# VectorE instead of GpSimd forms the low parts of the weights in the linear stages, and areas move to multiples of 512 bytes

## The chip, the cores and the metric

The kernel runs on one core of one Trainium2 chip. The metric is the device time of one execution in microseconds, taken as the median of several executions. Four engines compute: TensorE (PE, with its weight loads as PEld), VectorE (DVE), ScalarE (ACT) and GpSimd (POOL). SyncE (SP) issues the loads of the weights.

## The reference, cut to what matters

Two transformer-like blocks run one after the other on x of 512 tokens by 1024 features, in float32. Each has RMS norm, an input projection, mixers, an output projection that is added to x, a second norm, and a feed-forward part. Block one mixes by pooling and sparse attention, block two by a gated delta rule and banded attention. The stages on which the change acts are these:

```
# block one
h = rms_norm(x, ffn_norm_g)
gate_pre, val = split(h @ w_up, 2)                  # 1024 -> 2 x 2816
x = x + (silu(causal_dwconv(gate_pre, conv_w, conv_b)) * val) @ w_down
# block two
h = rmsnorm(x, norm_mix_w);  proj = h @ w_in
qkv = silu(causal_dwconv_2(concat([qa, ka, va]), conv_qkv_w))      # 4 taps
...
x = x + mix @ w_out
h = rmsnorm(x, norm_ffn_w)
u = causal_dwconv_2(h @ w_up, conv_ffn_w) + conv_ffn_b             # 3 taps, gate and value
gate, up = split(u, 2)
x = x + (silu(gate) * up) @ w_down
```

## The kernel before, in words

Activations lie with the features on the 128 partitions and the 512 tokens along the free dimension. Every product with a weight is made of three products of the faster float32r type: both the weight and the activation are split in a high and a low part, and high x high, high x low and low x high are summed in PSUM (lines 1452 to 1454, each a 128x128 weight slice against 128x512).

The weights come in 228 chunks, each the 8 slices (11 in the down projections) that make one output tile or half of one. w_raw, w_hi and w_lo have two slots each. For a chunk c, SyncE loads w_raw once w_lo of chunk c - 2 is made (line 508, the function load); ScalarE copies it to w_hi once TensorE is done with chunk c - 2 (semaphore chunk_done, line 679); GpSimd subtracts w_lo = w_raw - w_hi (line 590, the function low, semaphore lo_ready); TensorE waits for lo_ready and multiplies. Everybody prepares chunk c + 2 behind chunk c (the function ahead). While TensorE multiplies chunk c + 1, both parts of chunk c + 2 have to be made.

The stages and their numbers of chunks stand in the list STAGES: in1 15 and fill1 16 (input projection of block one, the latter interleaved with attention), mix1 8, out1 8, up1 44 (22 tiles of a gate chunk and a value chunk), down1 16 (8 tiles of two large chunks), in2c 12 (the convolution stage), in2z 5, fill2 28 (interleaved with the delta rule and attention), mix2 8, out2 8, up2 44, down2 16. In the trace up1 is 421 to 663 us, in2c 786 to 858, in2z 858 to 888 and up2 1316 to 1584. The tiles run in hardware loops of two tiles per iteration; the first two and the last two or so of a stage are unrolled.

What VectorE does behind a chunk, by the order of its instruction stream:

- up stages (function ffn): for the gate chunk it multiplies the bank by rms_inv into t_raw (line 1012), then applies three taps into t_gate (TENSOR_SCALAR at 1068, the second step at 1070, the third at 1073). In up1 the value chunk is only multiplied (into t_val); in up2 it gets the same convolution into t_val. Then t_gate x t_val (line 1089) once ScalarE has made the silu of t_gate, and act_lo = t_gate - act_hi (line 995) once ScalarE has made act_hi.
- in2c: multiplied by rms_inv into cv_raw, then four taps into cv (1288, 1291 three times); ScalarE makes the silu.
- out and down stages (function residual): adds the bank to X, makes h_lo (line 1001) and adds the square to sq_sum (line 1008), both behind ScalarE.
- mix stages (function merge): two gate products, their sum, and mix_lo behind ScalarE's mix_hi.
- in2z: multiplies by rms_inv (copy_tiles).

TensorE waits, apart from lo_ready, for a bank to be read (conv_done, cv_done, x_done). Behind the first chunk of a norm's stage it makes the mean of squares; ScalarE turns it into rms_inv, for which VectorE waits before its first multiplication.

Buffers in SBUF are placed by hand: weights, X, h_hi, h_lo, constants and parameters first, and then an arena in which the areas of the stages overlap.

Of the kernel before, what the change touches and what calls it, by code (L numbers as in the profile page):

```python
# [24 lines left out]
ALU = mybir.AluOpType  # L25
# [3 lines left out]
P = 128  # L29
T = 512  # L30
D = 1024
DK = D // P
# [117 lines left out]
def lin(a, b, i):  # L150

    return a + b * i if isinstance(i, int) else i * b + a
# [39 lines left out]
def two_blocks(nc, t_in, out):  # L192
# [10 lines left out]
    with ctx:  # L203
        kb = 1024
        base = -(-nc.sbuf_base // 64) * 64

# [7 lines left out]
        at = 0  # L214
# [10 lines left out]
        rms_inv = sb("rms_inv", [P, T], F32, at); at += T * 4  # L225
        arena = at
        arena_size = (nc.sbuf_usable_end - base - arena) // 64 * 64
# [260 lines left out]
        def ahead(c, q_kt):  # L488
# [4 lines left out]
            return (Chunk(n, 0, 0, None, False), SIZES[n]) if n < NCHUNK else (None, 0)  # L493

        def wait(eng, s, value):
            if not isinstance(value, int) or value > 0:
                eng.wait_ge(s, value)
# [88 lines left out]
        def _(pool):  # L586
            def low(c, kt):

                pool.wait_ge(hi_ready, c.count(1))
                pool.tensor_tensor(w_lo[:, c.slot, 0:kt * P], w_raw[:, c.slot, 0:kt * P],  # L590
                                   w_hi[:, c.slot, 0:kt * P], ALU.subtract).then_inc(lo_ready, 1)

            def split(name):
                n, per, kt = INFO[name]
                for i, j in units(pool, n):
                    for q in range(per):
                        c2, kt2 = ahead(chunk(name, i, j, q), kt)
                        if c2:
                            low(c2, kt2)

            def lows(name, plan, total):

                state = [0]

                def serve(*at):
                    upto = (plan[at][0] if at else total) // PIECES
                    while state[0] < upto:
                        low(*ahead(chunk(name, state[0] // 2, state[0] % 2), DK))
                        state[0] += 1
                return serve  # L610

            low(Chunk(0, 0, 0, None, False), DK)
            low(Chunk(1, 0, 0, None, False), DK)
            split("in1")
            pool.wait_ge(copied["in1"], 15)
# [19 lines left out]
            serve()  # L635
            for name in ("mix1", "out1", "up1", "down1", "in2c", "in2z"):
                split(name)
            pool.wait_ge(copied["in2z"], 5)
            pool.memset(gb_rows[:, :], 0.0).then_inc(blk_zero, 1)
            serve = lows("fill2", FILL2, FILLED2)  # L640
# [27 lines left out]
            serve()  # L668
            for name in ("mix2", "out2", "up2", "down2"):
                split(name)  # L670

# [321 lines left out]
        def _(dve):  # L993
# [34 lines left out]
            def residual(name, n):  # L1028
                per = INFO[name][1]
                for i, j in units(dve, DK):  # L1030
                    m = lin(j, 2, i)
                    dve.wait_ge(chunk_done, chunk(name, i, j, per - 1).count(1))
                    dve.tensor_tensor(X[:, m, :], X[:, m, :], bank(ACC + j), ALU.add).then_inc(x_done, 1)  # L1033
                    gained(n, m, j, isinstance(i, int) and m == 0)

            def copy_tiles(name, dst):
                for i, j in units(dve, INFO[name][0]):
                    dve.wait_ge(chunk_done, chunk(name, i, j).count(1))
                    scaled(dst[:, lin(j, 2, i), :], bank(ACC + j)).then_inc(copied[name], 1)

            def merge(name, b, sg, mt, mix_hi, mix_lo):
                for i, j in units(dve, DK):
                    m = lin(j, 2, i)
# [8 lines left out]
                    wait(dve, mix_hl[b], m)  # L1052
                    dve.tensor_tensor(mt[:, 2, :], mt[:, 0, :], mt[:, 1, :], ALU.add).then_inc(mixed[b], 1)
                    dve.wait_ge(mix_hh[b], lin(j + 1, 2, i))
                    sub(mix_lo[:, m, :], mt[:, 2, :], mix_hi[:, m, :]).then_inc(mix_hl[b], 1)

            def ffn(name, b, steps):
# [18 lines left out]
                for i, j in units(dve, FK):  # L1076
                    f = lin(j, 2, i)
                    val = t_val[:, j, :]
                    dve.wait_ge(chunk_done, chunk(name, i, j, 0).count(1))
                    conv(t_gate[:, j, :], bank(ACC), t_raw[:, 0, :], f, steps * j, i, j)  # L1080
                    dve.wait_ge(chunk_done, chunk(name, i, j, 1).count(1))
                    if b == 0:
                        wait(dve, gated[b], lin(j - 1, 2, i))
                        scaled(val, bank(ACC + 1)).then_inc(conv_done[b], 1)
                    else:
                        conv(val, bank(ACC + 1), t_raw[:, 1, :], lin(FK + j, 2, i), steps * j + 4, i, j)
                    dve.wait_ge(conv_done[b], lin(steps * j + steps, 2 * steps, i))
                    dve.wait_ge(silu_done[b], lin(j + 1, 2, i))
# [191 lines left out]
            for i, j in units(dve, 12):  # L1280
# [8 lines left out]
                for k in range(1, 4):  # L1289
                    dve.wait_ge(cv_done, lin(5 * j + k + 1, 10, i))  # L1290
                    dve.scalar_tensor_tensor(dst[:, k:], raw[:, 0:T - k], taps[:, t, 3 - k:4 - k], dst[:, k:],  # L1291
                                             ALU.mult, ALU.add).then_inc(cv_done, 1)
            copy_tiles("in2z", p2a[:, 12:17, :])

# [670 lines left out]
```

## Time and profile before

| what | value |
|---|---|
| median of 3 runs | 1731.11 us |
| lowest, highest | 1723.51, 1732.45 us |
| the profiled execution | 1725.94 us |
| its span, first to last instruction | 1724.0 us |
| TensorE, VectorE, ScalarE, GpSimd busy | 94%, 58%, 33%, 37% |
| mean granted clock of TensorE | 0.99 |
| w_lo subtractions on GpSimd | 228, 588.6 us busy |
| w_hi copies on ScalarE | 228, 250.4 us busy |

Engines work in parallel and meet at semaphores. Matmuls are pipelined: each 128x512 one is shown as some 0.39 us, while the next starts 0.23 us after it, so a TensorE that is shown 100% busy is one that never pauses. What an engine waited for stands in brackets behind a row. A granted clock of 1.00 is 2.4 GHz, 0.50 is 1.2 GHz.

### The profile page before, as it was taken

The numbers are of one execution on the slowest core, as the hardware profiler recorded it, in microseconds if no ns is written. First come the engines' busy times: TensorE is split into PE (matmuls) and PEld (weight loads), VectorE is DVE, ScalarE is ACT, GpSimd is POOL, SyncE is SP. The second block draws the span as 40 slices with busy tenths as digits, with TensorE's granted clock in tenths as the row PEclk, the third lists the DMA queues.
The fourth block names the chain that finished last, engine by engine and source line by source line (L and its number), as shares of the span: only waits on it lengthen the run. The fifth ranks groups of instructions, "written<-read, shape, count | busy, mean of one in ns | idle before, by whom it ended". The sixth has DMA issues, their size and how long they took to land.

```text
span 1724.0 us, 21757 instructions
## 1 busy us (share of the span) xinstructions
PE 1628.1 (94%) x7872; PEld 1277.9 (74%) x7872; DVE 995.8 (58%) x1295; ACT 568.8 (33%) x906; POOL 641.3 (37%) x274
## 2 busy tenths in 40 slices
PE   6997899999999999999999999999999999998997
PEld 4876666678888887887776798666688777777885
DVE  5146566576777775326924732245566888888223
ACT  5132455544322222223234223135444222222221
POOL 3452211144444444443433541131244444443432
PEclk9998999999999999999999999999999999999998
DMA  6421212142222223222222211252232222223231
GB/s 225 156 87 55 67 56 71 60 161 96 98 97 95 93 96 109 98 83 86 86 92 92 74 38 37 78 208 82 98 137 96 85 85 85 85 85 104 84 101 66
DMA packets 49845, 163.10 MB, mean 95 GB/s; under 512 B 5088, under 2 KB 5352, under 8 KB 49648
## 3 DMA queue, kind: packets, MB, share of 16 engines
q1 hardware_dynamic: 46544, 156.09, 26.4%
q10 hardware_dynamic: 3232, 6.08, 1.0%
q8 instruction: 44, 0.72, 0.2%
q14 instruction: 25, 0.20, 0.0%
HBM read 148.50 MB, written 13.65 MB: 94 GB/s over the span
## 4 chain that ended last, share of the span: by engine, by line
PE 69%; DVE 20%; issue 5%; ACT 4%; DVEq 1%; POOL 0%; DMA 0%; ACTq 0%
PE banks L1452 19%; PE banks L1454 18%; PE banks L1453 18%; DVE t_val L1073 3%; DVE t_gate L1068 3%; DVE cv L1291 2%; DVE t_raw L1012 2%; PE banks L1543 2%; PE banks L1569 2%; PE banks L1552 1%; DVE t_gate L1070 1%; PE banks L1773 1%; PE banks L1762 1%; DVE t_val L1070 1%; DVE t_gate L1089 1%
## 5 line engine op out<-in xcount | busy, mean ns | idle before, releaser
L590 POOL TENSOR_TENSOR w_lo<-w_raw,w_hi 128x1024 fp32r<-128x1024 f32 (+1 forms) x228 | 588.6, 2581 | 1020.8 <-ACT w_hi L679 1020.8
L1452 PE MATMUL banks<-h_hi,w_hi 128*128 128x512 f32 x1312 | 535.8, 408 | 49.6 <-POOL w_lo L590 31.5
L1454 PE MATMUL banks<-h_hi,w_lo 128*128 128x512 f32 x1312 | 514.2, 392 | 0.0
L1453 PE MATMUL banks<-h_lo,w_hi 128*128 128x512 f32 x1312 | 513.8, 392 | 0.0
L679 ACT ACTIVATE w_hi<-w_raw 128x1024 fp32r<-128x1024 f32 (+1 forms) x228 | 250.4, 1098 | 432.4 <-PE banks L1454 397.5
L1452 PEld LDWEIGHTS banks<-h_hi,w_hi 128*128 128x128 f32 x1312 | 247.6, 189 | 127.0 <-issue 53.0
L1454 PEld LDWEIGHTS banks<-h_hi,w_lo 128*128 128x128 f32 x1312 | 247.4, 189 | 53.5
L1453 PEld LDWEIGHTS banks<-h_lo,w_hi 128*128 128x128 f32 x1312 | 247.8, 189 | 51.2 <-issue 4.8
L1452 PE MATMUL banks<-act_hi,w_hi 128*128 128x512 f32 x352 | 140.7, 400 | 4.1 <-DVE t_raw L1012 3.2
L1453 PE MATMUL banks<-act_lo,w_hi 128*128 128x512 f32 x352 | 140.2, 398 | 0.0
L1454 PE MATMUL banks<-act_hi,w_lo 128*128 128x512 f32 x352 | 140.1, 398 | 0.0
L1033 DVE TENSOR_TENSOR X<-X,banks 128x512 f32<-128x512 f32 (+1 forms) x32 | 22.0, 687 | 176.4 <-PE banks L1454 176.4
L1068 DVE TENSOR_SCALAR t_gate<-t_raw,params 128x512 f32<-128x512 f32 x44 | 94.2, 2140 | 11.9 <-DVE t_raw L1012 11.6
L744 ACT ACTIVATE t_gate<-t_gate 128x512 f32<-128x512 f32 x44 | 27.8, 633 | 196.7 <-DVE t_gate L1073 196.7
L1001 DVE SCALAR_TENSOR_TENSOR h_lo<-X,params,h_hi 128x512 fp32r<-128x512 f32 (+1 forms) x32 | 71.1, 2221 | 36.4 <-ACT h_hi L718 36.4
L995 DVE TENSOR_TENSOR act_lo<-t_gate,act_hi 128x512 f32 (+1 forms) x44 | 66.7, 1515 | 39.2 <-ACT act_hi L747 39.2
L1452 PEld LDWEIGHTS banks<-act_hi,w_hi 128*128 128x128 f32 x352 | 66.8, 190 | 21.1 <-DVE t_raw L1012 3.6
L778 ACT ACTIVATE at_p<-at_sm,cols 128x128 f32<-128x128 f32 (+3 forms) x96 | 53.2, 555 | 87.0 <-DVE cols L1108 49.5
L1454 PEld LDWEIGHTS banks<-act_hi,w_lo 128*128 128x128 f32 x352 | 66.8, 190 | 16.3
L1453 PEld LDWEIGHTS banks<-act_lo,w_hi 128*128 128x128 f32 x352 | 66.9, 190 | 16.0
L1073 DVE SCALAR_TENSOR_TENSOR t_val<-t_raw,params,t_val 128x510 f32<-128x510 f32 x22 | 59.5, 2704 | 2.8
L747 ACT ACTIVATE act_hi<-t_gate 128x512 f32 (+1 forms) x44 | 27.8, 632 | 96.7 <-DVE t_gate L1089 96.7
(273 smaller groups left out, 1988.7 us busy)
## 6 DMA issues: line engine op xcount, KB each, us to landing
w_raw<-in_w_up SPq DMA_DIRECT2D x88, 512.0 KB, 3.4
w_raw<-in_w_fill SPq DMA_DIRECT2D x44, 512.0 KB, 3.5
w_raw<-in_w_down SPq DMA_DIRECT2D x32, 704.0 KB, 4.0
late_scratch<-stage SPq DMA_DIRECT2D x44, 256.0 KB, 2.1
w_raw<-in_w_mix SPq DMA_DIRECT2D x16, 512.0 KB, 4.3
sg<-late_scratch SPq DMA_DIRECT2D x16, 512.0 KB, 3.8
w_raw<-in_w_out SPq DMA_DIRECT2D x16, 512.0 KB, 3.5
w_raw<-in_w_in SPq DMA_DIRECT2D x15, 512.0 KB, 3.5
```

The source lines that it names most:

```text
L590: pool.tensor_tensor(w_lo[:, c.slot, 0:kt * P], w_raw[:, c.slot, 0:kt * P], w_hi[:, c.slot, 0:kt * P], ALU.subtract).then_inc(lo_ready, 1)
L679: act.activation(w_hi[:, c.slot, 0:kt * P], w_raw[:, c.slot, 0:kt * P], ACT.Copy)\
L778: act.activation(a.p[:, s % 2, half, 0:w], a.sm[:, half, 0:w], ACT.Exp, bias=a.nbias[:, c:c + 1], scale=DH ** -0.5, accum_out=a.sums[:, c: ...
L995: return dve.tensor_tensor(out_, a, b, ALU.subtract)
L1001: dve.scalar_tensor_tensor(h_lo[:, m, :], X[:, m, :], gains[:, m + DK * n, :], h_hi[:, m, :], ALU.mult, ALU.subtract).then_inc(hl_done, 1)
L1012: return dve.tensor_tensor(dst, src, rms_inv[:, :], ALU.mult)
L1068: dve.tensor_scalar(dst, raw, w(2), w(3), ALU.mult, ALU.add).then_inc(conv_done[b], 1)
L1070: dve.scalar_tensor_tensor(dst[:, 1:], raw[:, 0:T - 1], w(1), dst[:, 1:], ALU.mult, ALU.add)\
L1073: dve.scalar_tensor_tensor(dst[:, 2:], raw[:, 0:T - 2], w(0), dst[:, 2:], ALU.mult, ALU.add)\
L1452: pe.matmul(dst, w_h, hi[:, kr, :], start=first and n == 0, stop=False)
L1453: pe.matmul(dst, w_h, lo[:, kr, :], start=False, stop=False)
L1454: mm = pe.matmul(dst, w_l, hi[:, kr, :], start=False, stop=last and n == len(ks) - 1)
```

## The change

The function low, which subtracts, becomes one that can be issued on either engine, and next_low issues the one for the chunk two ahead. In in1, fill1 and fill2 it stays with GpSimd, and so do the first two chunks behind each fill stage. In mix1, out1, up1, down1, in2c, in2z, mix2, out2, up2 and down2 VectorE issues it: behind the convolution or the multiplication of the chunk, in residual behind sq_sum (and for all but a tile's last chunk, before the bank is awaited), in merge between the sum and mix_lo. These are 169 of the 228 subtractions. merge on VectorE now begins with a wait until GpSimd's two subtractions for the first two mix chunks are made, and GpSimd waits before it clears gb_rows until VectorE's for the first two fill2 chunks are made. The number of each kind of operation stays the same. Apart from this, the first buffer and the arena begin at multiples of 512 bytes instead of 64.

```diff
-        base = -(-nc.sbuf_base // 64) * 64
+        base = -(-nc.sbuf_base // 512) * 512
...
-        arena = at
+        arena = at = -(-at // 512) * 512
...
+        def low(eng, c, kt):
+
+            eng.wait_ge(hi_ready, c.count(1))
+            eng.tensor_tensor(w_lo[:, c.slot, 0:kt * P], w_raw[:, c.slot, 0:kt * P],
+                              w_hi[:, c.slot, 0:kt * P], ALU.subtract).then_inc(lo_ready, 1)
+
+        def next_low(eng, name, i, j, q=0):
+            c2, kt2 = ahead(chunk(name, i, j, q), INFO[name][2])
+            if c2:
+                low(eng, c2, kt2)
...
-            for name in ("mix1", "out1", "up1", "down1", "in2c", "in2z"):
-                split(name)
             pool.wait_ge(copied["in2z"], 5)
+            pool.wait_ge(lo_ready, BASE["fill2"] + 2)
             pool.memset(gb_rows[:, :], 0.0).then_inc(blk_zero, 1)
...
-            for name in ("mix2", "out2", "up2", "down2"):
-                split(name)
...
                 for i, j in units(dve, DK):
                     m = lin(j, 2, i)
+                    for q in range(per - 1):
+                        next_low(dve, name, i, j, q)
                     dve.wait_ge(chunk_done, chunk(name, i, j, per - 1).count(1))
                     dve.tensor_tensor(X[:, m, :], X[:, m, :], bank(ACC + j), ALU.add).then_inc(x_done, 1)
                     gained(n, m, j, isinstance(i, int) and m == 0)
+                    next_low(dve, name, i, j, per - 1)
...
             def merge(name, b, sg, mt, mix_hi, mix_lo):
+                dve.wait_ge(lo_ready, BASE[name] + 2)
...
                     dve.tensor_tensor(mt[:, 2, :], mt[:, 0, :], mt[:, 1, :], ALU.add).then_inc(mixed[b], 1)
+                    next_low(dve, name, i, j)
...
                     conv(t_gate[:, j, :], bank(ACC), t_raw[:, 0, :], f, steps * j, i, j)
+                    next_low(dve, name, i, j, 0)
...
                         conv(val, bank(ACC + 1), t_raw[:, 1, :], lin(FK + j, 2, i), steps * j + 4, i, j)
+                    next_low(dve, name, i, j, 1)
...
                     dve.scalar_tensor_tensor(dst[:, k:], raw[:, 0:T - k], taps[:, t, 3 - k:4 - k], dst[:, k:],
                                              ALU.mult, ALU.add).then_inc(cv_done, 1)
-            copy_tiles("in2z", p2a[:, 12:17, :])
+                next_low(dve, "in2c", i, j)
+            copy_tiles("in2z", p2a[:, 12:17, :], True)
```

## Rows read from the trace of the kernel before

**Rows 1.** The page's first part, busy time (share of the span) xinstructions by engine.
```profile
PE 1628.1 (94%) x7872; PEld 1277.9 (74%) x7872; DVE 995.8 (58%) x1295; ACT 568.8 (33%) x906; POOL 641.3 (37%) x274
```

**Rows 2.** Busy by stage: PE, PEld, DVE, ACT, POOL; then granted clock, DMA.
```profile
421.00:663.00 242.00, 241.06 (x1062) 198.93 (x1061) 187.79 (x155) 75.45 (x94) 106.92 (x44) 1.00 0.29 97
...
786.00:858.00 72.00, 69.25 (x292) 53.73 (x290) 61.94 (x59) 22.89 (x29) 31.13 (x12) 1.00 0.24 82
858.00:888.00 30.00, 29.48 (x123) 24.22 (x124) 8.28 (x10) 6.62 (x8) 12.03 (x5) 0.94 0.29 95
...
1316.00:1584.00 268.00, 248.16 (x1058) 195.25 (x1056) 220.65 (x218) 74.31 (x94) 115.12 (x44) 1.00 0.26 88
```

**Rows 3.** Timeline: start us, duration us, instruction, idle before; VectorE, one tile.
```profile
1432.21 0.68 DVE L1012 TENSOR_TENSOR t_raw<-banks,rms_inv 128x512 f32<-128x512 f32 x1
...
1437.82 0.55 DVE L1068 TENSOR_SCALAR t_val<-t_raw,params 128x512 f32<-128x512 f32 x1 [0.28 <-DVE t_raw L1012]
...
1439.41 2.63 DVE L1073 SCALAR_TENSOR_TENSOR t_val<-t_raw,params,t_val 128x510 f32<-128x510 f32 x1
1442.17 0.69 DVE L1089 TENSOR_TENSOR t_gate<-t_gate,t_val 128x512 f32<-128x512 f32 x1
1443.79 0.69 DVE L995 TENSOR_TENSOR act_lo<-t_gate,act_hi 128x512 f32 x1 [0.93 <-ACT act_hi L747]
1444.40 0.68 DVE L1012 TENSOR_TENSOR t_raw<-banks,rms_inv 128x512 f32<-128x512 f32 x1
```

**Rows 4.** The same timeline, GpSimd, beside the rows of group 3.
```profile
1438.64 2.86 POOL L590 TENSOR_TENSOR w_lo<-w_raw,w_hi 128x1024 fp32r<-128x1024 f32 x1 [3.78 <-ACT w_hi L679]
```

**Rows 5.** The same timeline, TensorE, starts of two chunks.
```profile
1441.63 0.49 PE L1452 MATMUL banks<-h_hi,w_hi 128*128 128x512 f32 x1 [0.87 <-POOL w_lo L590]
...
1447.19 0.48 PE L1452 MATMUL banks<-h_hi,w_hi 128*128 128x512 f32 x1
```

**Rows 6.** Groups by form: xcount, busy us, mean ns; window 1344:1576.
```profile
L590 POOL TENSOR_TENSOR w_lo<-w_raw,w_hi 128x1024 fp32r<-128x1024 f32 x39 | 102.1, 2618 | 134.9 <-ACT w_hi L679 134.9
...
L1073 DVE SCALAR_TENSOR_TENSOR t_val<-t_raw,params,t_val 128x510 f32<-128x510 f32 x20 | 53.0, 2649 | 2.7
...
L1068 DVE TENSOR_SCALAR t_gate<-t_raw,params 128x512 f32<-128x512 f32 x19 | 37.0, 1949 | 5.8 <-DVE t_raw L1012 5.8
...
L1073 DVE SCALAR_TENSOR_TENSOR t_gate<-t_raw,params,t_gate 128x510 f32<-128x510 f32 x19 | 14.3, 750 | 2.8 <-DVE t_gate L1070 2.7
...
L1068 DVE TENSOR_SCALAR t_val<-t_raw,params 128x512 f32<-128x512 f32 x19 | 10.4, 547 | 5.0 <-DVE t_raw L1012 5.0
```

**Rows 7.** Groups by form, whole span: one VectorE operation at two sizes.
```profile
L1104 DVE CUSTOM_DVE_ANT_0 at_sm<-banks,consts 128x512 f32<-128x512 f32 x16 | 10.4, 687 | 10.0 <-PE banks L1552 10.0
...
L1104 DVE CUSTOM_DVE_ANT_0 at_sm<-banks,consts 128x384 f32<-128x384 f32 x16 | 8.4, 554 | 2.1 <-PE banks L1552 2.0
```

**Rows 8.** Timeline, first up projection: a chunk's last matmul, and VectorE behind it.
```profile
569.11 0.39 PE L1454 MATMUL banks<-h_hi,w_lo 128*128 128x512 f32 x1
...
569.62 0.69 DVE L1012 TENSOR_TENSOR t_raw<-banks,rms_inv 128x512 f32<-128x512 f32 x1 [0.70 <-PE banks L1454]
```

**Rows 9.** Timeline, convolution stage: TensorE at the start of two chunks.
```profile
803.91 0.49 PE L1452 MATMUL banks<-h_hi,w_hi 128*128 128x512 f32 x1 [0.28 <-POOL w_lo L590]
...
809.76 0.49 PE L1452 MATMUL banks<-h_hi,w_hi 128*128 128x512 f32 x1
```

**Rows 10.** Timeline, TensorE at three stage ends; then two windows as in group 2.
```profile
662.92 0.50 PE L1452 MATMUL banks<-act_hi,w_hi 128*128 128x512 f32 x1 [0.94 <-DVE t_val L1012]
...
858.52 0.50 PE L1452 MATMUL banks<-h_hi,w_hi 128*128 128x512 f32 x1 [1.84 <-DVE cv_raw L1012]
...
1584.04 0.79 PE L1452 MATMUL banks<-act_hi,w_hi 128*128 128x512 f32 x1 [3.20 <-DVE t_raw L1012]
...
1584.00:1589.00 5.00, 4.96 (x12) 3.89 (x13) 4.91 (x3) 1.31 (x2) 3.18 (x1) 0.50 0.18 70
663.00:668.00 5.00, 5.00 (x22) 4.05 (x23) 3.94 (x2) 1.72 (x2) 3.23 (x1) 1.00 0.34 133
```

More of the change, by code:

```diff
@@ L586, in _ @@
         def _(pool):
[L587 to L599, printed above, removed]
             def lows(name, plan, total):
@@ L607, in serve @@
                     while state[0] < upto:
-                        low(*ahead(chunk(name, state[0] // 2, state[0] % 2), DK))
+                        next_low(pool, name, state[0] // 2, state[0] % 2)
                         state[0] += 1
                 return serve
-            low(Chunk(0, 0, 0, None, False), DK)
-            low(Chunk(1, 0, 0, None, False), DK)
-            split("in1")
+            low(pool, Chunk(0, 0, 0, None, False), DK)
+            low(pool, Chunk(1, 0, 0, None, False), DK)
+            for i, j in units(pool, INFO["in1"][0]):
+                next_low(pool, "in1", i, j)
             pool.wait_ge(copied["in1"], 15)
@@ L1034, in residual, with copy_tiles @@
                     gained(n, m, j, isinstance(i, int) and m == 0)
-            def copy_tiles(name, dst):
+                    next_low(dve, name, i, j, per - 1)
+            def copy_tiles(name, dst, lows=False):
                 for i, j in units(dve, INFO[name][0]):
@@ L1039, in copy_tiles @@
                     scaled(dst[:, lin(j, 2, i), :], bank(ACC + j)).then_inc(copied[name], 1)
+                    if lows:
+                        next_low(dve, name, i, j)
             def merge(name, b, sg, mt, mix_hi, mix_lo):
+                dve.wait_ge(lo_ready, BASE[name] + 2)
                 for i, j in units(dve, DK):
@@ L1053, in merge @@
                     dve.tensor_tensor(mt[:, 2, :], mt[:, 0, :], mt[:, 1, :], ALU.add).then_inc(mixed[b], 1)
+                    next_low(dve, name, i, j)
                     dve.wait_ge(mix_hh[b], lin(j + 1, 2, i))
```

## The prediction, made before the result was known

> **What bounds the kernel now.** I read the busy shares on the page first [rows 1]: TensorE is busy 94% of the span of 1724.0 us, VectorE 58%, GpSimd 37%, ScalarE 33%. So a change on VectorE and GpSimd can only pay, or cost, where TensorE is made to wait. The table by stage [rows 2] says where that is. In the first up projection TensorE is busy 241.1 of 242.0 us; there nothing can be won. In the second up projection (1316 to 1584 us) it is idle for 19.8 us of 268.0, and VectorE is busy 220.7 us, 82%; in the convolution stage (786 to 858) TensorE is idle 2.8 of 72.0 us and VectorE busy 86%. About as many matmuls (1062 and 1058) take 242 us in the first up projection and 268 us in the second. Those 26 us are the stake.
>
> The timeline of VectorE over one tile of the second up projection [rows 3] shows why. From one t_raw to the t_raw two later (1432.21 to 1444.40) is 12.19 us, and VectorE is never idle for more than the latency of its own dependences, except 0.93 us before act_lo. 22 such tiles are 268.2 us: the stage runs at VectorE's pace. In that tile the last t_val instruction took 2.63 us; GpSimd's w_lo ran from 1438.64 to 1441.50 [rows 4], and the t_val instruction ended 0.54 us after it. The groups by form [rows 6] show that this is the rule: that same operation has a mean of 2649 ns on t_val, and TENSOR_SCALAR takes 1949 ns on t_gate and 547 ns on t_val, with equal shapes. The slow ones are those that meet a w_lo subtraction. An instruction that reads PSUM beside rms_inv (line 1012) keeps 0.68 to 0.69 us throughout. TensorE in turn waits at every second chunk for GpSimd's w_lo: 0.87 us idle before the matmul at 1441.63 [rows 5].
>
> **What is removed.** 169 of the 228 subtractions leave GpSimd. In a tile of the second up projection VectorE gets back 1949 - 547 = 1.40 us on t_gate and 2649 - 750 = 1.90 us on t_val (750 ns is the same step's mean on t_gate, which meets no w_lo [rows 6]). 12.19 - 3.30 = 8.89 us.
>
> **What is added.** Two subtractions of 128x1024 a tile on VectorE, an operation that the trace has nowhere at this size. Its nearest rows: TENSOR_TENSOR with both inputs in SBUF and 512 elements takes 0.69 us (1442.17 and 1443.79 in rows 3), and a VectorE instruction grows by 687 - 554 = 133 ns for 128 elements [rows 7], 1.04 ns an element. 0.69 + 512 x 1.04 ns = 1.22 us. Its bounds: not under 0.69 us (half the size), not over 2.62 us, GpSimd's own mean in this stage [rows 6]. I take 1.22, since the rows of 512 elements are the same operation on the same engine and from the same memory. For 1408 elements it is 1.62 us. Independent VectorE instructions start 0.08 us before the one ahead has ended (t_raw at 1444.40 behind act_lo), so one adds 1.14 us; and as one now stands between t_val and the product t_gate x t_val, 0.13 + 0.08 = 0.21 us of dependence latency goes. VectorE's own tile: 8.89 + 2.28 - 0.21 = 10.96 us.
>
> The Trainium skill, VectorE: DVE Perf Modes, section on the TRN2 errata, has a table of 58 cycles plus one an element for SBUF operands, 1.13 us for 1024 elements, which would take 0.18 us more off the tile and 4 us off the kernel; by that table 512 elements take 0.59 us, and the rows have 0.69, so the measurement decides against it.
>
> **The new path.** w_lo now stands behind the convolution in VectorE's order, and TensorE waits for it. From a chunk's t_raw, in the looped code: TENSOR_SCALAR 0.68 + 0.28 = 0.96 later, the third step 1.59 after that (1437.82 to 1439.41) with 0.75 of work when it isn't stretched [rows 3, 6], in all 3.30 us; the subtraction starts 0.08 before that, at 3.22, and ends at 4.44, and TensorE starts 0.13 later (1441.50 in rows 4 to 1441.63 in rows 5): 4.57. A chunk that began with a stall is followed by the next 5.56 us after (1441.63 to 1447.19 [rows 5]), and ends 5.72 us after its start, 0.16 after the next one's start (5.60 where no stall went before). VectorE starts 0.12 after the chunk's end (569.11 + 0.39 to 569.62 [rows 8]). The loop that now binds runs over two tiles: t_raw of the gate half, its w_lo, TensorE's gate chunk and value chunk, VectorE's value half with its subtraction, product and act_lo (3.22 + 1.14 + 1.62 + 0.61 = 6.59): 4.57 + 5.56 + 5.60 + 0.12 + 6.59 = 22.44, so 11.22 us a tile. TensorE alone needs 242/22 = 11.0 [rows 2], VectorE alone 10.96. All three lie close together: the stage becomes nearly balanced.
>
> **Sum for the second up projection.** The first two tiles are unrolled, and I leave them. 20 tiles give 20 x (12.19 - 11.22) = 19.4 us. At its end TensorE waits 3.20 us for VectorE's late t_raw (1584.04 [rows 10]); at the end of the first up projection, where VectorE is in time, it is 0.94 us (662.92). By then VectorE runs in time here too, but most of that difference is the lag that the last tiles carry, already in the 12.19; I count 0.6. Together 20.0 us. Behind that wait the granted clock is 0.50 from 1584 to 1589 [rows 10], 1.2 GHz instead of 2.4; after the 0.94 us wait it stays at 1.00. 12 matmuls pass in those 5 us instead of 22; over the 6.8 us or so until the clock is back that is 14 matmuls at 0.42 instead of 0.23, 2.7 us, which I round to 2.8 with the pipelined edges. I expect the drop to go with the wait: 2.8 us more, or nothing as the other bound.
>
> **The convolution stage.** Chunks start 5.85 us apart (803.91 and 809.76 [rows 9]). After: 0.12 + 4.57 and one more step of 0.90, less 0.05 for a shorter TENSOR_SCALAR, make 5.54 us from a chunk's end to TensorE's start on the one two later, with 5.72 for the chunk itself 11.26 for two, 5.63 each. Ten chunks give 2.2 us. The wait of 1.84 us at its end (858.52 [rows 10]) shrinks to about 0.94: 0.9 won, and with it a clock drop of the same kind: the 30 us behind it have a mean clock of 0.94 [rows 2], some 1.6 us. Together 4.7.
>
> **Edits that I cost at nothing.** First up projection: TensorE sets the pace, VectorE still waits 0.70 us for TensorE in each tile [rows 8]. The gate half's w_lo is ready 0.12 + 4.57 = 4.69 us after its chunk's end, and TensorE wants it at 5.3 (242/44 = 5.5 a chunk, less the overlap of 0.16); the cover is 0.6 us, and every 0.1 us beyond costs 22 x 0.1 = 2.2 us. One cost there is not nothing: in these stages the first convolution waits for rms_inv, and now the first w_lo waits with it. None of my rows prices that; VectorE's wait can push it out by 0 to 2 us at each of the three stages. I take 1.0 for the three together, since all but the rms_inv wait itself fits in the chunk's 5.3 us. Output and down projections: after the tile's last chunk VectorE does X, h_lo and sq_sum, three operations of 0.69 to 0.75 us [rows 3, 6] with a wait for ScalarE's w_hi and h_hi between, then the subtraction; I estimate it ready at 4.6 us of 5.3, and at 5.4 of 7.5 us for the large chunks (11 slices instead of 8). Merge: the subtraction waits for w_hi, and behind it in VectorE's queue stand mix_lo and the next gate product; that product ends some 4 us after the chunk, TensorE asks for it at 5.3. The load of w_raw on SP's queue waits for w_lo, which comes no later than it did by more than a microsecond, with a whole chunk of cover. New waits: merge begins with a VectorE wait for GpSimd's last two w_lo, with the first gate product behind it, wanted by TensorE a chunk (5.5 us) later: 0 to 1 us, I take 0. GpSimd's wait before gb_rows ends with VectorE's last subtraction of the z stage, before it has other work: 0. The attention and delta-rule stages keep GpSimd's subtractions and their times.
>
> The arena moves from 448 to 0 modulo 512 bytes against the weights (3774 constants and 427 parameters of 4 bytes, each rounded up to 64). Line 1012 into t_raw, in the arena, has its 0.68 us, the same as the other 512-element operations; no row distinguishes an address, so 0, with a gain as likely as a loss.
>
> **Sum.** 20.0 + 2.8 + 4.7 - 1.0 = 26.5 us off the profiled execution: 1725.9 becomes 1699.4. That execution was 5.2 us under the median of 1731.1 (runs from 1723.5 to 1732.5), so against the median I say 1704.6.
>
> **Rivals.** (a) Most of the gain is lost: the subtraction takes 1.5 to 1.8 us or the waits in front of it are not hidden. VectorE's tile is 10.96 + 2 x (L - 1.22); at L = 1.5 both limits are 11.5, the stage gives 14 us, the clock and the convolution stage 5: 1712. At L = 1.83 the tile is 12.19 again, the convolution stage gives 1, and the kernel is at 1730. For it: the size is unseen in the trace. Against: both neighbours lie on one line.
> (b) Slower: VectorE needs for the subtraction what GpSimd needed, 2.62 us [rows 6]. The place is the path from a chunk's end over the convolution to w_lo. In the first up projection it becomes 0.12 + 5.97 + 5.72 = 11.8 a tile against 11.0, 18 us; in the second VectorE's 13.76 against 12.19, 35 us; in the convolution stage (5.54 + 1.40 + 5.72)/2 = 6.3 a chunk against 5.85, 5 us; the clock drops stay: 1731 + 58 = 1789. It decides from L = 1.83 us on.
> (c) The stretch on VectorE isn't GpSimd's doing and stays; VectorE, 82% busy, gets 2.28 us a tile on top: 12.19 + 2.28 - 0.21 = 14.26 us, 46 us in the second up projection. In the first, with t_gate stretched by 1.40 us, the path is 0.12 + 4.57 + 1.40 + 5.72 = 11.8 against 11.0, 18 us: 1795. The rows speak against it, since only instructions that lie under a w_lo are long.
> The Trainium skill, Perfetto Trace Analysis, section Optimizing Scalar/DVE Operations, has the rule behind (c): with VectorE saturated, move work away from it, to ScalarE or even GpSimd. It adds that between those two this might not help, as they share a read port of SBUF.
> (d) Better: TensorE alone binds both stages (11.0 a tile): 26 + 2.8 + 6 = 35, 1696, and with a median as low as the profiled run 1691.
>
> **Chances.** Forecast 0.64, its own range 1697 to 1712; (d) 0.07; (a) 0.17, of which 0.12 lies under 1722; (b) 0.05, (c) 0.03; the rest, 0.04, is something unforeseen of about no change. The range 1691 to 1722 holds about 8 in 10 with the doubt on the clock drops (5 us) and on the median (4 us). Half a percent, 8.7 us, is about what a measurement of this kernel can tell from no change: faster is below 1722.4, 0.83; same 0.09; slower 0.08.
>
> **What would show it.** In the changed trace: 128x1024 w_lo on VectorE at 1.22 us; t_gate's TENSOR_SCALAR and t_val's last step at 0.55 and 0.75; tiles of 11.2 us in the second up projection, and 11.0 still in the first; waits of about 1 us at the ends of the up and convolution stages and a clock of 1.00 behind them. If w_lo is at 1.22 and the first up projection has grown, the cover of 0.6 us was not there; if t_gate stays at 1.9, (c) holds.

## The result and the profile after

| | before | after |
|---|---|---|
| median of the runs | 1729.45 us (4 runs) | 1684.51 us (4 runs, 1683.65 to 1689.85) |
| ratio | | 0.9751, 95% interval 0.9716 to 0.9785 |
| profiled execution, its span | 1725.94, 1724.0 us | 1683.67, 1681.9 us |

The changed kernel is 45 us faster by the medians, 42.1 us by the two spans. 1704.6 was forecast, and 1691 was the lower end of the range. Runs of one kernel differ by several us, since TensorE's clock drops at some of its pauses in one run and not in the next (last section). The busy shares of the page, after, beside [rows 1]:

```profile
PE 1604.2 (95%) x7872; PEld 1275.3 (76%) x7872; DVE 931.2 (55%) x1462; ACT 577.4 (34%) x906; POOL 201.7 (12%) x107
```

167 subtractions are new on VectorE (61 of the 228 stayed with GpSimd, so two fewer moved than the 169 that the description of the change and the prediction give), and it is busy for 64.6 us less. The table by stage, after, with the columns of [rows 2]:

```profile
375.00:419.00 44.00, 44.00 (x196) 36.44 (x195) 25.09 (x32) 17.06 (x23) 0.00 (x0) 1.00 0.29 93
419.00:660.00 241.00, 240.76 (x1060) 198.49 (x1058) 156.42 (x199) 79.19 (x94) 0.00 (x0) 1.00 0.30 98
660.00:780.00 120.00, 119.45 (x527) 98.92 (x528) 40.78 (x40) 30.21 (x31) 0.00 (x0) 1.00 0.29 97
780.00:850.00 70.00, 68.25 (x293) 54.19 (x291) 53.96 (x71) 25.18 (x30) 0.00 (x0) 1.00 0.26 83
...
1301.00:1548.00 247.00, 244.50 (x1060) 197.10 (x1058) 195.28 (x262) 78.20 (x94) 0.00 (x0) 1.00 0.30 95
```

The second up projection has come down from 268 to 247 us, and the first has its 241 as before. That is the part that was foreseen. The first down projection (third row) is the part that wasn't: 120 us. In the kernel before the same stage and the output projection ahead of it were these rows of the table by stage, which the prediction did not show:

```profile
376.00:421.00 45.00, 45.00 (x194) 36.27 (x193) 28.64 (x25) 17.06 (x23) 19.33 (x8) 1.00 0.28 95
663.00:786.00 123.00, 123.00 (x528) 99.12 (x529) 34.72 (x23) 30.07 (x31) 50.86 (x16) 1.00 0.28 95
```

TensorE was busy for all of the 123 us, it waited for nobody, and yet the stage has become 3.4 us shorter.

VectorE's timeline over one tile of the second up projection, after, answers to [rows 3]:

```profile
1442.62 0.69 DVE L1007 TENSOR_TENSOR t_raw<-banks,rms_inv 128x512 f32<-128x512 f32 x1
1443.68 0.55 DVE L1070 TENSOR_SCALAR t_gate<-t_raw,params 128x512 f32<-128x512 f32 x1 [0.37 <-DVE t_raw L1007]
...
1445.95 1.22 DVE L498 TENSOR_TENSOR w_lo<-w_raw,w_hi 128x1024 fp32r<-128x1024 f32 x1
1447.09 0.68 DVE L1007 TENSOR_TENSOR t_raw<-banks,rms_inv 128x512 f32<-128x512 f32 x1
...
1449.64 0.75 DVE L1075 SCALAR_TENSOR_TENSOR t_val<-t_raw,params,t_val 128x510 f32<-128x510 f32 x1
1450.30 1.22 DVE L498 TENSOR_TENSOR w_lo<-w_raw,w_hi 128x1024 fp32r<-128x1024 f32 x1
1451.44 0.68 DVE L1093 TENSOR_TENSOR t_gate<-t_gate,t_val 128x512 f32<-128x512 f32 x1
1453.05 0.69 DVE L990 TENSOR_TENSOR act_lo<-t_gate,act_hi 128x512 f32 x1 [0.93 <-ACT act_hi L742]
1453.66 0.68 DVE L1007 TENSOR_TENSOR t_raw<-banks,rms_inv 128x512 f32<-128x512 f32 x1
```

The tile is 11.04 us here instead of 12.19 (over the stage 247.4 / 22 = 11.2), w_lo takes 1.22 us, t_gate's TENSOR_SCALAR 0.55 and t_val's last step 0.75. From about 1424 us on TensorE waits once for each pair of tiles, at every fourth chunk, and from one such wait to the next it is 22.49 us (1447.30 to 1469.79). The waits at the ends of the stages have shrunk, where [rows 5] and [rows 10] had 0.87, 0.94, 1.84 and 3.20 us:

```profile
1447.30 0.49 PE L1457 MATMUL banks<-h_hi,w_hi 128*128 128x512 f32 x1 [0.35 <-DVE w_lo L498]
...
1469.79 0.49 PE L1457 MATMUL banks<-h_hi,w_hi 128*128 128x512 f32 x1 [0.39 <-DVE w_lo L498]
...
660.55 0.50 PE L1457 MATMUL banks<-act_hi,w_hi 128*128 128x512 f32 x1 [0.78 <-DVE t_val L1007]
...
850.03 0.50 PE L1457 MATMUL banks<-h_hi,w_hi 128*128 128x512 f32 x1 [0.78 <-DVE cv_raw L1007]
...
1548.56 0.50 PE L1457 MATMUL banks<-act_hi,w_hi 128*128 128x512 f32 x1 [0.78 <-DVE t_raw L1007]
...
1549.00:1554.00 5.00, 5.00 (x24) 4.10 (x23) 4.23 (x6) 0.89 (x2) 0.00 (x0) 1.00 0.42 140
```

The last row is the window behind the second up projection: clock 1.00, where [rows 10] had 0.50.

Stage by stage, from the first matmul of a stage to the first of the next, in us. The last columns are experiments of the next section:

| stage | before | after | e1 VectorE, old addresses | e2 new addresses alone | e8 earlier subtraction |
|---|---|---|---|---|---|
| mix1 | 45.2 | 43.6 | 46.4 | 45.7 | 43.6 |
| out1 | 44.8 | 43.5 | 44.8 | 43.5 | 43.5 |
| up1 | 241.4 | 241.4 | 241.4 | 241.4 | 241.2 |
| down1 | 123.3 | 119.9 | 123.3 | 119.8 | 119.9 |
| in2c | 72.3 | 69.6 | 69.7 | 72.2 | 67.1 |
| in2z | 29.0 | 27.4 | 27.3 | 27.3 | 27.4 |
| mix2 | 46.8 | 43.7 | 46.3 | 44.6 | 43.7 |
| out2 | 44.8 | 43.5 | 44.8 | 43.5 | 43.5 |
| up2 | 268.3 | 247.4 | 247.4 | 268.2 | 243.1 |
| down2 and end | 139.9 | 133.3 | 137.7 | 135.0 | 133.3 |

### The profile page after: what moved, and what is told of

The parts are those of the page before. It is cut to its first block, busy times and chain, and to the rows that moved or that the text cites. A ratio compares the mean times of both kernels' runs of the same rounds, so it can differ in the third digit from the quotient of the medians.

```text
span 1681.9 us, 21641 instructions
## 1 busy us (share of the span) xinstructions
PE 1604.2 (95%) x7872; PEld 1275.3 (76%) x7872; DVE 931.2 (55%) x1462; ACT 577.4 (34%) x906; POOL 201.7 (12%) x107
## 4 chain that ended last, share of the span: by engine, by line
PE 83%; DVE 9%; issue 4%; ACT 3%; POOL 0%; DVEq 0%; DMA 0%; ACTq 0%
PE banks L1457 23%; PE banks L1459 23%; PE banks L1458 23%; PE banks L1548 2%; PE banks L1574 2%; PE banks L1557 1%; PE banks L1778 1%; PE banks L1767 1%; PE banks L1631 1%; ACT at_pt L782 1%; PE banks L1762 1%; ACT at_p L773 1%; DVE w_lo L498 1%; PE banks L1820 1%; DVE t_raw L1007 1%
## 5 line engine op out<-in xcount | busy, mean ns | idle before, releaser
L498 DVE TENSOR_TENSOR w_lo<-w_raw,w_hi 128x1024 fp32r<-128x1024 f32 (+1 forms) x167 | 216.7, 1297 | 79.2 <-ACT w_hi L674 79.0
L498 POOL TENSOR_TENSOR w_lo<-w_raw,w_hi 128x1024 fp32r<-128x1024 f32 x61 | 149.0, 2443 | 432.1 <-ACT w_hi L674 432.1
L1457 PE MATMUL banks<-act_hi,w_hi 128*128 128x512 f32 x352 | 137.2, 390 | 1.6 <-DVE t_val L1007 0.8
L1459 PE MATMUL banks<-act_hi,w_lo 128*128 128x512 f32 x352 | 136.9, 389 | 0.0
L1030 DVE TENSOR_TENSOR X<-X,banks 128x512 f32<-128x512 f32 (+1 forms) x32 | 22.0, 688 | 99.6 <-PE banks L1459 99.6
L1007 DVE TENSOR_TENSOR t_raw<-banks,rms_inv 128x512 f32<-128x512 f32 x66 | 45.5, 689 | 33.9 <-PE banks L1459 27.0
L1574 PEld LDWEIGHTS banks<-at_pt,v_nat 128*64 128x64 f32 x480 | 25.6, 136 | 38.8 <-ACT at_pt L782 30.0
```

The source lines that it names most:

```text
L498: eng.tensor_tensor(w_lo[:, c.slot, 0:kt * P], w_raw[:, c.slot, 0:kt * P], w_hi[:, c.slot, 0:kt * P], ALU.subtract).then_inc(lo_ready, 1)
L1007: return dve.tensor_tensor(dst, src, rms_inv[:, :], ALU.mult)
L1457: pe.matmul(dst, w_h, hi[:, kr, :], start=first and n == 0, stop=False)
L1459: mm = pe.matmul(dst, w_l, hi[:, kr, :], start=False, stop=last and n == len(ks) - 1)
L1574: mm = pe.matmul(banks[rows(half), BO + j % 2, i * P:(i + 1) * P], v_tile(j, b, half, k), a.pt[:, half, k * P:(k + 1) * P], start=opens an ...
```

## Experiments

**The two halves of the change.** e1 is the changed kernel with these two lines put back, e2 the kernel before with them alone:

```diff
-        base = -(-nc.sbuf_base // 512) * 512
+        base = -(-nc.sbuf_base // 64) * 64
...
-        arena = at = -(-at // 512) * 512
+        arena = at
```

> VectorE subtracts, but the first buffer and the arena begin where they did before. Theory A (the address: moving operands of TensorE that lie in the arena are read more slowly from an address of 64 modulo 128 bytes; 1824 matmuls of the down, output and mix stages at 233 instead of 227 ns): 12 us slower than the changed kernel, 1684.5 + 12 = 1696.5, matmul starts 233 ns apart on act, mix, yp, o, oa and ob, 227 on h. Theory B (GpSimd's subtraction slows TensorE in these stages and the address does nothing): 1684.5 and 227 ns throughout.

> The kernel before with the two address lines alone. Theory A: 12 us faster than before, 1729.5 - 12 = 1717.5, arena matmuls at 227 ns. Theory B: no difference, 1729.5, arena matmuls at 233 ns.

Measured, beside the kernel before at 1727.2 us: e1 1703.2 us, ratio 0.9862 (0.9835 to 0.9888). e2 1717.1 us, ratio 0.9939 (0.9919 to 0.9960). So VectorE's subtraction is worth 24 us, and the addresses, for which nothing had been counted, 10 us on the kernel before. Where the second part lies is seen in two windows of 100 us without any wait, the first in the first down projection, whose moving operand act lies in the arena, the second in the first up projection, whose operand h doesn't. Before:

```profile
670.00:770.00 100.00, 100.00 (x430) 80.57 (x429) 26.21 (x18) 24.77 (x25) 42.00 (x13) 1.00 0.27 92
500.00:600.00 100.00, 100.00 (x443) 82.84 (x442) 77.66 (x65) 30.05 (x38) 44.51 (x19) 1.00 0.28 94
```

e1, and behind it e2:

```profile
670.00:770.00 100.00, 100.00 (x430) 80.60 (x429) 32.57 (x31) 24.74 (x25) 0.00 (x0) 1.00 0.28 92
500.00:600.00 100.00, 100.00 (x443) 82.81 (x442) 65.05 (x83) 31.34 (x38) 0.00 (x0) 1.00 0.29 95
```

```profile
670.00:770.00 100.00, 100.00 (x443) 82.84 (x442) 27.95 (x19) 24.75 (x25) 43.13 (x14) 1.00 0.29 94
```

430 matmuls against 443 in the same time at the same clock: 233 ns from one to the next instead of 226 (the last row is e2's first window). GpSimd has nothing to do with it, since e1 is slow without its subtractions and e2 fast with 14 of them in the window. Theory B is out.

**Which address.** Four experiments moved the blocks against each other; a fifth of the same kind, with both at 64, is e4. All are the changed kernel with such an edit, here e3 and e5. e6 and e7 have 128 and 256 in the place of e3's 64, and e4 has e5's first line alone, with which the arena moves along:

```diff
-        arena = at = -(-at // 512) * 512
+        arena = at = -(-at // 512) * 512 + 64
```

```diff
-        base = -(-nc.sbuf_base // 512) * 512
+        base = -(-nc.sbuf_base // 512) * 512 + 64
...
-        arena = at = -(-at // 512) * 512
+        arena = at = -(-at // 512) * 512 + 448
```

> The changed kernel with the arena alone moved on by 64 bytes; weights and h stay at 0 modulo 512. Theory A: 1696.5, arena matmuls at 233 ns, h at 227. Theory B: 1684.5. Rival within A, that the old base of the weights matters: then this one stays near 1684.5 too.

> The changed kernel with everything, weights, h and arena, moved on by 64 bytes. Theory A with the operand's own address: h is slow too, 3936 + 1824 matmuls at 6.6 ns, 38 us: 1722. Theory A with the distance between operand and weights: no difference, 1684.5. Theory B: 1684.5.

> The changed kernel with weights and h at 64 modulo 512 and the arena back at 0: no operand has the address that it has in the slow kernels but the distance from weights to arena is 448 modulo 512 as in the kernel before. Theory C (the distance between the weights that TensorE loads and the moving operand that it reads decides): arena matmuls at 233 ns, 12 us slower than the changed kernel, 1696.5. Theory A (an operand's own address decides, with the arena at a multiple of 512): 227 ns and 1684.5.

> The changed kernel with the arena moved on by 128 bytes, weights at 0. Theory C with any distance that is not a multiple of 512: 233 ns again, 1696.5. Rival: only distances that are no multiple of 128 cost something: 227 ns, 1684.5.

> As before with 256 bytes. Theory C with any distance that is not a multiple of 512: 233 ns, 1696.5. Rival that multiples of 256 suffice: 227 ns, 1684.5.

| kernel | weights and h, bytes mod 512 | arena, mod 512 | distance | one matmul to the next on act | time of one execution |
|---|---|---|---|---|---|
| before, e1, e12 | 128 | 64 | 448 | 233.3 ns | |
| e5 | 64 | 0 | 448 | 233.3 ns | 1699.4 us |
| e6 | 0 | 128 | 128 | 233.3 ns (mix2 and out2 232.4) | 1698.6 us |
| e3 | 0 | 64 | 64 | 228.9 ns (mix1 and out1 233.3) | 1699.5 us |
| e7 | 0 | 256 | 256 | 226.8 ns | 1688.4 us |
| e4 | 64 | 64 | 0 | 226.8 ns | 1686.6 us |
| after, e2 | 0 | 0 | 0 | 226.8 ns | |

The intervals are means over the matmuls of the traces that follow each other without a pause. e3 to e7 are single executions, and e3's holds eight drops of the clock where the others have two or three; so its intervals and not its time say what a distance of 64 costs. The window in the first down projection says the same; e3, e4, e5, e6 and e7 in this order:

```profile
670.00:770.00 100.00, 100.00 (x438) 82.07 (x437) 34.49 (x34) 25.39 (x26) 0.00 (x0) 1.00 0.28 94
```

```profile
670.00:770.00 100.00, 100.00 (x443) 82.81 (x442) 35.39 (x35) 25.89 (x27) 0.00 (x0) 1.00 0.28 92
```

```profile
670.00:770.00 100.00, 100.00 (x430) 80.60 (x429) 32.58 (x31) 24.75 (x25) 0.00 (x0) 1.00 0.27 90
```

```profile
670.00:770.00 100.00, 100.00 (x431) 80.42 (x430) 32.58 (x31) 24.75 (x25) 0.00 (x0) 1.00 0.27 92
```

```profile
670.00:770.00 100.00, 100.00 (x443) 82.84 (x442) 33.26 (x32) 26.39 (x27) 0.00 (x0) 1.00 0.28 92
```

e4 sinks the theory that I went in with, that an operand at 64 is slow by itself: everything lies at 64 there and everything is fast. e5 is its counterpart: the arena is at a multiple of 512, as in the changed kernel, and slow again. What decides is the distance between the block of the weights and that of the moving operand. Distances of 0 and 256 cost nothing; 448 costs 6.6 ns a matmul, 128 as much (5.7 in mix2 and out2), and 64 costs 2 ns in four of the stages and 6.6 in mix1 and out1, so the rule isn't complete. The expectation for e7, that only multiples of 512 are free, missed, and so did e6's rival, that multiples of 128 are.

Does another engine that works in the weights' block collide with TensorE's reads? The traces answer that: in e1's first down projection 46 matmuls start while VectorE, ScalarE and GpSimd stand still and no DMA packet is under way, and they are 233.2 ns apart; 45 such in the changed kernel are 226.6 ns apart. So TensorE loses the time with nobody beside it. That the two reads which meet are the moving rows of one matmul and the weights of the next fits all of this, but it is argued: no experiment separates the two reads.

**Is 12 us all of it?** By stage the addresses give 3.4 us in down1, 3.5 in down2 (136.9 us in e12 against 133.4 in e11), and 1.2 to 1.3 in each of mix1, out1, mix2 and out2: 1824 matmuls at 6.6 ns, 12.0 us. In the traces compared for this (e12 and e5 against the changed kernel) no drop of the clock falls into the stage, but for the last one, which every trace has; e1's 46.4, 46.3 and 137.7 us in the table above hold more than the addresses. The first medians (1703.2 and 1684.5) were 18.7 apart, so both kernels ran again on one chip, the changed kernel six times and the one with old addresses five:

> The changed kernel once more, beside the two others of this call: 1684 to 1688.

> VectorE subtracts, old addresses, once more. By the stages of the traces the addresses are worth 12 us (1824 matmuls at 6.6 ns). If that is all, this one is 12 us above the changed kernel of this call; if the 18.7 us of the first medians (1703.2 and 1684.5) are real, the addresses have a second effect.

Measured: the changed kernel 1689.0 (ratio 0.9775, 0.9748 to 0.9803), with old addresses 1700.7 (0.9838, 0.9814 to 0.9862). They are 11.6 apart, so no second effect is seen. The other 7 us go with drops of the clock, which came and went (last section): the trace of e1 has five of 1.7 us each, that of the changed kernel none.

**What stretched VectorE.** In e10 GpSimd subtracts constants into an area that nobody uses, behind each w_hi of the second up projection:

```diff
...
+            for i, j in units(pool, FK):
+                for q in range(2):
+                    pool.wait_ge(hi_ready, chunk("up2", i, j, q).count(3))
+                    wait(pool, spared[1], lin(2 * j + q, 4, i))
+                    pool.tensor_tensor(spare[:, :], consts[:, 0:2 * T], consts[:, 2 * T:4 * T], ALU.subtract)\
+                        .then_inc(spared[1], 1)
```

> The changed kernel with a subtraction of 128x1024 on GpSimd (constants, into an unused area) behind each w_hi of the second up projection, where nobody waits for its result. Theory (GpSimd's subtraction is what stretches VectorE's instructions, whatever it is for): VectorE's steps grow by the 3.3 us a tile that they had before, 11.0 + 3.3 = 14.3 us a tile, 314 us instead of 247: 1751. Rival (the stretch came from the shared w_raw and w_hi, or from the semaphores): 247 us and 1684.

Measured: 1756.4 us in a single execution, the stage 313.8 us. Groups by form in that stage, columns as in [rows 6], and from the timeline one instruction of GpSimd with the TENSOR_SCALAR of VectorE that meets it, two times:

```profile
L501 DVE TENSOR_TENSOR w_lo<-w_raw,w_hi 128x1024 fp32r<-128x1024 f32 x36 | 43.9, 1218 | 0.0
L1079 DVE TENSOR_SCALAR t_val<-t_raw,params 128x512 f32<-128x512 f32 x18 | 43.6, 2424 | 5.0 <-DVE t_raw L1016 5.0
L1079 DVE TENSOR_SCALAR t_gate<-t_raw,params 128x512 f32<-128x512 f32 x18 | 35.8, 1988 | 5.4 <-DVE t_raw L1016 5.4
```

```profile
L673 POOL TENSOR_TENSOR spare<-consts 128x1024 f32<-128x1024 f32 x36 | 86.1, 2392 | 171.2 <-ACT w_hi L683 171.2
```

```profile
1427.80 2.39 POOL L673 TENSOR_TENSOR spare<-consts 128x1024 f32<-128x1024 f32 x1 [5.60 <-ACT w_hi L683]
1428.63 1.85 DVE L1079 TENSOR_SCALAR t_gate<-t_raw,params 128x512 f32<-128x512 f32 x1 [0.37 <-DVE t_raw L1016]
...
1434.06 2.39 POOL L673 TENSOR_TENSOR spare<-consts 128x1024 f32<-128x1024 f32 x1 [3.86 <-ACT w_hi L683]
1434.31 2.43 DVE L1079 TENSOR_SCALAR t_val<-t_raw,params 128x512 f32<-128x512 f32 x1 [0.28 <-DVE t_raw L1016]
```

Nobody waits for GpSimd here and it touches nothing that VectorE works on, and the TENSOR_SCALAR steps are 2424 and 1988 ns instead of 546. So GpSimd's subtraction holds them up, whichever data it takes. The Trainium skill, SBUF — State Buffer, section Who interferes with whom, says that VectorE and GpSimd share one pair of ports as a lock, and that one who comes second waits for the whole instruction. The trace agrees: one TENSOR_SCALAR begins 0.83 us and the other 0.25 us after GpSimd's instruction, and both end 0.29 us behind its end (1430.48 and 1430.19, 1436.74 and 1436.45). The 43 stretched ones of the run all end 0.28 to 0.29 us behind. So it is the time left of GpSimd's instruction that sets whether 1.4 or 1.9 us are added. What the prediction gives from the Trainium skill with rival (c), on two engines that share a read port, is about this pair, VectorE and GpSimd.

**How much VectorE can take.** e9 puts one more subtraction of 128x1024 (constants, into an unused area) ahead of each w_lo of both up projections:

```diff
...
+                    wait(dve, spared[b], lin(2 * j + 0, 4, i))
+                    dve.tensor_tensor(spare[:, :], consts[:, 0:2 * T], consts[:, 2 * T:4 * T], ALU.subtract)\
+                        .then_inc(spared[b], 1)
                     next_low(dve, name, i, j, 0)
...
```

> The changed kernel with one more subtraction of 128x1024 (constants, into an unused area) on VectorE ahead of each w_lo in both up projections. By the steps of the prediction, the second up projection then goes at VectorE's own pace, 11.0 + 2 x 1.14 = 13.2 us a tile, 291 us instead of 247; the first at the path over w_lo, 0.12 + 4.57 + 1.14 + 5.72 = 11.55 us a tile, 254 us instead of 241.4: 1684 + 57 = 1741. Rival, that VectorE has slack in the first up projection: 241.4 there, and 1728.

Measured: 1745.2 us in a single execution; 256.7 us in the first up projection and 289.8 in the second.

```profile
420.00:677.00 257.00, 246.75 (x1061) 197.25 (x1060) 202.22 (x243) 79.84 (x94) 0.00 (x0) 1.00 0.28 91
1319.00:1609.00 290.00, 255.49 (x1061) 202.01 (x1059) 243.67 (x305) 77.22 (x94) 0.00 (x0) 0.97 0.26 81
```

The sums of the prediction gave 254 and 291. The cover of the first up projection is as thin as was counted, or thinner: 1.14 us more on the path cost it 15.3 us, 0.70 a tile, though VectorE is busy for only 79% of it. That leaves 0.44 us of cover where 0.6 was put.

**A better order.** The same sums say that TensorE's remaining wait is the path over the convolution. e8 issues w_lo behind the first tap instead of behind the whole convolution, in both up projections and in the convolution stage:

```diff
                     dve.tensor_scalar(dst, raw, w(2), w(3), ALU.mult, ALU.add).then_inc(conv_done[b], 1)
+                    next_low(dve, name, i, j, q)
...
                     conv(t_gate[:, j, :], bank(ACC), t_raw[:, 0, :], f, steps * j, i, j, 0)
-                    next_low(dve, name, i, j, 0)
```

> The changed kernel with the subtraction moved forward: behind the first tap (TENSOR_SCALAR) instead of behind the whole convolution, in both up projections and in the convolution stage. Theory (the path of a chunk's end over the convolution to w_lo is what still holds TensorE): w_lo is ready 2.9 instead of 4.6 us after the chunk, the second up projection goes from 247.4 to TensorE's own 241.4 us, the convolution stage from 69.6 to 67: 8 us faster than the changed kernel, 1676. Rival: the silu and w_hi of ScalarE come later by the 1.1 us of the subtraction and VectorE's own pace of some 11 us a tile binds: no difference, 1684.

> The earlier subtraction once more: by its stages (4.3 us in the second up projection, 2.5 in the convolution stage) 6 to 7 us under the changed kernel of this call. If the drops of the clock vary more than that, the medians don't separate.

e13 is the same kernel again. Measured: 1681.7 us (ratio 0.9732, 0.9705 to 0.9759), and the second time, beside the changed kernel's 1689.0, 1684.9 (0.9747, 0.9724 to 0.9771). Inside the second up projection the profile shows no wait; at its end there is one:

```profile
1298.00:1541.00 243.00, 243.00 (x1065) 198.66 (x1063) 193.46 (x262) 74.19 (x92) 0.00 (x0) 1.00 0.30 97
```

```profile
1542.32 0.50 PE L1457 MATMUL banks<-act_hi,w_hi 128*128 128x512 f32 x1 [1.32 <-DVE t_raw L1007]
```

It is 243.1 us, the convolution stage 67.1: 4.3 and 2.5 us less than in the changed kernel, in both traces. By the medians of one chip it is 4.1 us ahead, and the intervals of the ratios overlap; by stage the gain of 6.8 us is plain, by the time of the whole it lies within what the clock takes or gives. It is the fastest version of this study. 241.4 was expected of the up projection, not 243.1, and 8 us of the whole. Against the 241.2 us of the first up projection, 0.5 us is the longer wait at the end (1.32 us, the first has 0.78); the rest is mostly in matmuls that start 0.07 to 0.1 us late from 1431 us on, too little to be shown as idle time.

## Why the prediction was right, and where it was wrong

**VectorE's subtraction: right.** With the old addresses, which is what the sum described, the kernel takes 1703.2 and 1700.7 us; 1704.6 was forecast. That is 24.0 and 28.3 us under the kernel before beside it, against 26.5 in the sum. The terms: w_lo 1.22 us forecast, 1.219 measured. A tile of the second up projection 11.22, measured 247.4 / 22 = 11.25; the loop over two tiles 22.44, measured 22.49, with the one wait for w_lo where the path puts it; 20.0 us off the stage, measured 20.9. The clock behind it 2.8; down2 with the end is 2.2 us shorter than before in e1 and 3.0 in e12, their addresses being the old ones. In that the size is partly luck: e2 has the same wait of 3.2 us there, and behind it 3.4 us at half the clock instead of the 6.8 of the kernel before. Convolution stage with its end 4.7 - 1.0 = 3.7, measured 2.7 + 1.6 = 4.3. The cost of the first w_lo behind rms_inv, for which I had no row, is there: 0.69 us of wait in the convolution stage, where about 1 us was put for all three. In the trace after:

```profile
793.03 0.49 PE L1457 MATMUL banks<-h_hi,w_hi 128*128 128x512 f32 x1 [0.69 <-DVE w_lo L498]
```

The first up projection kept its 241.4 us. Rivals (a) and (b) fell with w_lo's 1.22 us and (c) with the 0.55 us of the TENSOR_SCALAR; e10 shows that (c)'s 14.3 us a tile is what comes if the stretch stays (313.8 / 22 = 14.26). Rival (d), at 1691 to 1696, came nearest in time, but not by its cause: TensorE alone does not bind the second up projection, which still waits for w_lo at 11.25 us a tile instead of 11.0.

One reading in the prediction is off, without an effect on the sum. It set the 1.13 us of the table in the Trainium skill against the 1.22 us for which the instruction is shown. The next instruction starts 1.14 us after it (1445.95 and 1447.09), which is what the sum used, so the table would have changed the tile by 0.02 us, not 0.18, and the rows do not decide against it.

**The addresses: wrong, and this is the step that failed.** The prediction says: "no row distinguishes an address, so 0, with a gain as likely as a loss." The trace did distinguish one. I had looked at VectorE's instructions only, and compared their durations. TensorE's showed it: 528 matmuls in the 123.0 us of the first down projection are 233 ns each, 1062 in the 242.0 us of the first up projection 228, at the same clock, TensorE busy 100 and 99.6% of the time, with operands in two blocks that the change moves against each other. I took "busy without a pause" for "cannot become faster". The term was worth 12.0 us: 1824 matmuls by 6.6 ns. With it the sum would have been 38.5 us and the forecast 1692.6, inside the range, against 1689.0 and 1684.5 measured in two sets of runs; beside the kernel before the gain was 39.9 and 44.9 us.

**The rest.** 1684.5 was a sample from the low side: the same kernel had a median of 1689.0 in a second set of 6 runs, from 1683.4 to 1694.7. In the profiled execution after, no drop of the clock fell into the mix stages; before, one of 3.4 us stood at the start of mix2 and is in its 46.8 us. The range had room for such a draw or for a term of 12 us that nobody counted, not for both.

## What to carry to other kernels

An engine that is busy 100% of a stage isn't at its limit: compare the rate of the same instruction between stages, and look for what differs, here where the operand lies relative to the weights. For matmuls like these, which follow each other without a pause, place moving operands and weights at a distance that is a multiple of 256 bytes; of the five distances tried, 0 and 256 modulo 512 were the free ones. Before work is moved off GpSimd, count what its instructions add to VectorE's, since that can be more than the work itself (3.3 us a tile against 2.3 here), and put what the next engine waits for ahead of what nobody waits for.

## What the runs showed of the hardware that I had not expected

TensorE's own rate depends on the distance between two SBUF addresses. In detail, from the starts: at a distance of 0 or 256 nearly all intervals are 226 to 227 ns. At 448 they mostly alternate between 231 and 236, but in mix1 and out1 of e1 and e12, at the same addresses, they stay at 233 to 234. At 128 they lie between 229 and 238 on act, and at 64 they go 229, 232, 226 on act and stay at 233 to 234 in mix1 and out1. What chooses the pattern stays open. The Trainium skill says in SBUF — State Buffer, section Who interferes with whom, that PE never waits on anyone; these runs do not speak against that for other engines, but have TensorE lose 3% (233.3 against 226.8 ns) with the other engines and the DMA queues at rest.

The clock drops of 3.4 us are no fixed property of a schedule. Of the 60 in the traces, one of them 6.8 us long, 57 begin in or just behind a pause of TensorE of 1.4 us or more; three, in e3 and e4, have only pauses of 0.7 to 1.2 us before them. And not each long pause has one: the attention of block one has a pause of 1.6 us at about 210 us, in the changed kernel and in e11, which is the same kernel. Here are the row of that pause and the window around and behind it, first for the changed kernel, then for e11:

```profile
210.21 0.33 PE L1548 MATMUL banks<-consts,at_p 128*128 128x128 f32 x1 [1.60 <-DVE at_p L1126]
...
209.00:215.00 6.00, 4.79 (x26) 2.94 (x26) 5.02 (x18) 2.21 (x9) 1.08 (x1) 1.00 0.31 87
```

```profile
209.69 0.33 PE L1548 MATMUL banks<-consts,at_p 128*128 128x128 f32 x1 [1.59 <-DVE at_p L1126]
...
209.00:215.00 6.00, 5.31 (x22) 2.74 (x22) 3.84 (x18) 1.42 (x6) 0.55 (x1) 0.72 0.29 87
```

Each costs up to 1.7 us, and the traces have none (the changed kernel) to twelve (e10) of them beside the long one at 146 us and the last. That is most of the spread between runs of one kernel: the executions of 1683.4 and 1694.7 us have mean clocks of 0.994 and 0.987, and 0.7% of 1684 us is 11.8 us. What chooses among the pauses stays open. The waits of 0.78 us at the ends of stages, which the new order leaves, were not followed by a drop in any trace of the changed kernel; e9, which has pauses of 2.2 us in the second up projection, has five drops in it.
